# A mixing stage laid out anew: paired heads in the sparse attention, gate products between its steps, and no empty matmuls

## The reference

```python
u = rms_norm_2(h, mix_norm[i])
z = u @ w_in[i]
(aq, ak, av, iq, ik, iw, rq, rk, rv, rg, ga, gb) = jnp.split(z, split_points, axis=-1)
aq, ak, iq, ik = rope(...)                       # 8 heads of 64; ak, av, ik are one shared head
y_a = dsa_attention(aq, ak, av, iq, ik, iw, n_sel)
rq, rk = rope(...)                               # 4 heads of 128
y_r = group_norm_heads(retention(rq, rk, rv), ret_gn[i]) * jax.nn.silu(rg)
merged = jax.nn.sigmoid(ga) * (y_a @ w_branch_a[i]) + jax.nn.sigmoid(gb) * (y_r @ w_branch_b[i])
h = h + merged @ w_out[i]
```

## Time and profile before

| | us |
|---|---|
| median of the runs | 2613.55 (2613.17 to 2618.36, 3 runs) |
| span of the profiled execution | 2617.4 |
| slowest of the runs, with which that span agrees but for 1.0 | 2618.36 |
| PE busy in the profile | 2480.4 (95% of the span) |
| DVE busy | 1396.8 (53%) |
| ACT busy | 764.3 (29%) |
| POOL busy | 595.8 (23%) |

### The profile page before, as it was taken

The page is one execution under the profiler, slowest core; times in us unless marked ns, Lnnn a source line. Parts: engine busy times, 40 slices in busy tenths (PEclk is TensorE's granted clock), DMA queues, the critical chain, the costliest instruction groups (busy, mean ns, idle before and its releaser), DMA issues.

```text
span 2617.4 us, 29928 instructions
## 1 busy us (share of the span) xinstructions
PE 2480.4 (95%) x11088; PEld 1980.8 (76%) x11088; DVE 1396.8 (53%) x1951; ACT 764.3 (29%) x1204; POOL 595.8 (23%) x275
## 2 busy tenths in 40 slices
PE   6789999988999999999999999979989999999997
PEld 5677888876667788887888887566578887888886
DVE  5566444453676643446554357698435245544465
ACT  2114323321333432333322233412422113322232
POOL 6670000015446000000000005463036882000000
PEclk8899999998999999999999999989999999999999
DMA  4232333312223233332333322121012333333321
GB/s 163 73 96 65 113 97 96 97 48 80 80 72 97 65 107 102 96 98 68 106 96 98 95 82 80 41 72 48 16 39 75 96 112 91 115 101 95 86 81 53
DMA packets 64824, 221.81 MB, mean 85 GB/s; under 512 B 7504, under 2 KB 9680, under 8 KB 64592
## 3 DMA queue, kind: packets, MB, share of 16 engines
q1 hardware_dynamic: 59184, 208.17, 27.0%
q10 hardware_dynamic: 5536, 12.19, 1.4%
HBM read 218.23 MB, written 2.10 MB: 84 GB/s over the span
## 4 chain that ended last, share of the span: by engine, by line
PE 82%; DVE 11%; ACT 3%; POOL 2%; issue 2%; DMA 0%; POOLq 0%; ACTq 0%; DVEq 0%
PE PS L422 22%; PE PS L424 21%; PE PS L423 21%; PE PS L508 3%; PE PS L453 3%; PE PS L570 1%; PE PS L457 1%; DVE SS L1252 1%; POOL WL L367 1%; PE PS L584 1%; PE PS L805 1%; PE PS L717 1%; PE PS L605 1%; PE PS L738 1%; PE PS L727 1%
## 5 line engine op out<-in xcount | busy, mean ns | idle before, releaser
L422 PE MATMUL PS<-XH,WH 128*128 128x512 f32 x1600 | 633.4, 396 | 18.1 <-DVE T L1476 12.5
L424 PE MATMUL PS<-XH,WL 128*128 128x512 f32 x1632 | 637.0, 390 | 0.0
L423 PE MATMUL PS<-XL,WH 128*128 128x512 f32 x1600 | 624.1, 390 | 0.0
L364 POOL TENSOR_TENSOR WH<-RAW,ONES 128x1024 fp32r<-128x1024 f32 (+1 forms) x123 | 240.9, 1958 | 1569.8 <-DVE WL L1240 734.8
L1240 DVE TENSOR_TENSOR WL<-RAW,WH 128x1024 fp32r<-128x1024 f32 (+2 forms) x268 | 317.6, 1185 | 198.4 <-ACT WH L899 193.7
L422 PE MATMUL PS<-HH,WH 128*128 128x512 f32 x992 | 389.0, 392 | 2.6 <-DVE HL L1326 2.6
L424 PE MATMUL PS<-HH,WL 128*128 128x512 f32 x992 | 386.2, 389 | 0.0
L423 PE MATMUL PS<-HL,WH 128*128 128x512 f32 x992 | 386.1, 389 | 0.0
L422 PEld LDWEIGHTS PS<-XH,WH 128*128 128x128 f32 x1600 | 301.4, 188 | 98.3 <-issue 20.2
L899 ACT ACTIVATE WH<-RAW 128x1024 fp32r<-128x1024 f32 (+2 forms) x272 | 276.7, 1017 | 305.9 <-DVE M L1357 202.4
L424 PEld LDWEIGHTS PS<-XH,WL 128*128 128x128 f32 x1632 | 307.2, 188 | 64.9
(11 more groups left out here) (236 smaller groups left out, 2786.4 us busy)
## 6 DMA issues: line engine op xcount, KB each, us to landing
RAW<-in_weights SPq DMA_DIRECT2D x379, 512.0 KB, 3.5
RAW<-in_weights SPq DMA_DIRECT2D x16, 384.0 KB, 3.1
H<-in_xT ACTq DMA_DIRECT2D x8, 256.0 KB, 8.4
BIAS<-in_rel ACTq DMA_DIRECT2D x8, 256.0 KB, 3.5
RAW<-in_weights SPq DMA_DIRECT2D x8, 256.0 KB, 2.7
out<-R ACTq DMA_DIRECT2D x8, 256.0 KB, 2.1
BIAS<-in_rel ACTq DMA_DIRECT2D x8, 224.0 KB, 3.9
DECAY<-in_decay ACTq DMA_DIRECT2D x1, 1024.0 KB, 4.9
```

Source lines behind the costliest of these rows:

```text
L364: nc.gpsimd.tensor_tensor(high[:, 0:w], raw, ONES[:, 0:1].to_broadcast([P, w]), ALU.mult).then_inc(high_split, 1)
L422: nc.tensor.matmul(PS[:, bank_, :], high[:, w], xh[:, k, :], start=(k == 0), stop=False)
L423: nc.tensor.matmul(PS[:, bank_, :], high[:, w], xl[:, k, :], start=False, stop=False)
L424: return nc.tensor.matmul(PS[:, bank_, :], low[:, w], xh[:, k, :], start=False, stop=stop)
```

## The change

It touches the mixing stage alone. What each part does now:

- **`mix_heads`**: no empty matmuls. DVE takes a unit straight out of PSUM times the cosine (`cosine_part`; 1/rms is multiplied into the four tables once, with four multiplications at the start), ACT copies crosswise straight out of PSUM, and the bank counts as evacuated only after the sine (`sine_part`). The index scores are done in pairs on the two halves of PE's rows, behind every second tile of the last five units (`index_pair`, `beside_heads`). ACT copies the scores into the search's work area.
- **`ret_qk`**: the crosswise halves lie in PSUM (`swapped`), and three rounds of the search go with each unit instead of two.
- **`ret_v`**: 15 rounds before the first half is taken out, 9 before the second. PE goes through the half bank by bank (`half_by_banks`), each bank waiting for its own evacuation alone.
- **The retention comes before the sparse attention**, written out without loops; PE reads `R1` directly (no `KR`), the next head's scores come before the transposes, and the output's high and low parts (`RH`, `RL`) are made per head.
- **The sparse attention** has the first attention's form: 16 steps of two heads, with four tiles of the 8 gate-a units (`merge_a`, now a table row of its own) in each. In each step ACT scales the first head's probabilities and DVE the second's.
- **`merge`** is left with 24 units: gate b, branch a, branch b.
- **Weights**: POOL's last range ends at unit 295. From there to 330 ACT and DVE split (`split_behind`, and the calls in the merge), four units ahead; the units from 323 on use `WH2`/`WL2`.

```diff
-            ("ret_gate", 8), ("merge", 32), ("mix_out", 8), ("ffn_b2", 2 * FFN_B + 8 * len(groups_of(FFN_B))),
+            ("ret_gate", 8), ("merge_a", 8), ("merge", 24), ("mix_out", 8), ("ffn_b2", 2 * FFN_B + 8 * len(groups_of(FFN_B))),
-POOL_RANGES = ((0, 28), (92, 124), (256, 331))
+POOL_RANGES = ((0, 28), (92, 124), (256, 295))
```

PE's list:

```diff
-            product(DT, XH, XL)
-            keep_busy(24, 7)
-            pe.wait_ge(evacuated, v_ready)
...
-            for t in range(TT):
-                product(DT, XH, XL, after=lambda k: index_scores(8 * t + k))
+            def index_pair(m):
+                t, a = divmod(m, PAIRS)
+                if m == 0:
+                    pe.wait_ge(rotated, 5)
+                if m == 1:
+                    pe.wait_ge(index_ready, 1)
+                if m >= 2:
+                    pe.wait_ge(relu_done, 2 * m - 2)
+                for hh in range(2):
+                    r = slice(hh * HD, hh * HD + HD)
+                    nc.tensor.matmul(PS[:, 4 + m % 2 * 2 + hh, 0:n_of(t)], AQIQ[r, 4 + a, t * P:t * P + P],
+                                     IK[r, 0:n_of(t)], start=True, stop=True).then_inc(index_done, 1)
+            def beside_heads(j):
+                if j == 1:
+                    transpose_avw()
+                if j % 2 == 1 and j // 2 < TT * PAIRS:
+                    index_pair(j // 2)
+            for s in range(5):
+                product(DT, XH, XL, after=lambda k: beside_heads(s * DT + k))
+            for s in range(8):
+                product(DT, XH, XL)
+            half_by_banks()
+            half_by_banks()
...
+            ret_scores(0)
+            for h in range(4):
+                ret_gate(2 * h)
+                ret_values(h)
+                ret_gate(2 * h + 1)
+                if h < 3:
+                    ret_scores(h + 1)
+                ret_transposes(h)
...
+            for s in range(first_step, last_step + 1):
+                j = 4 * (s - first_step)
+                if s < last_step:
+                    sparse_scores(s)
+                gate_a_tile(j)
+                gate_a_tile(j + 1)
+                if s > first_step:
+                    sparse_transposes(s - 1)
+                gate_a_tile(j + 2)
+                gate_a_tile(j + 3)
+                if s > first_step:
+                    sparse_values(s - 1)
```

ACT's list, in each step of the sparse attention:

```diff
+                for hh in range(2):
+                    c = s % 2 * 2 + hh
+                    act.wait_ge(x_done, 2 * s + hh + 1)
+                    x = PROB[:, s % 2, hh, 0:n_of(t)]
+                    S.activation(x, x, ACT.Exp, bias=NMX[:, c:c + 1], scale=-1.0,
+                                 accum_out=SUMX[:, c:c + 1]).then_inc(e_done, 1)
+                act.wait_ge(sums_inverted, s - first_step + 1)
+                c = s % 2 * 2
+                x = PROB[:, s % 2, 0, 0:n_of(t)]
+                S.activation(x, x, ACT.Copy, scale=RECX[:, c:c + 1]).then_inc(first_scaled, 1)
+                if t % 2 == 1 and s > first_step + 2:
+                    split_behind((s - first_step - 3) // 2)
```

DVE's list:

```diff
+            def cosine_part(n, cos, scale):
+                if n >= 2:
+                    dve.wait_ge(rotated, n - 1)
+                V.scalar_tensor_tensor(T[:, n % 2 * 2, :], unit(), scale, cos, ALU.mult, ALU.mult).then_inc(turned, 1)
+            def sine_part(n, dst, sin, scale):
                 dve.wait_ge(act_out, ao.next())
+                V.scalar_tensor_tensor(swapped(n), swapped(n), scale, sin, ALU.mult, ALU.mult).then_inc(evacuated, 1)
+                dve.wait_ge(evacuated, FIRST["mix_heads"] + n + 1 + (n > 4) + SLOTS)
+                V.tensor_tensor(dst, swapped(n), T[:, n % 2 * 2, :], ALU.add).then_inc(rotated, 1)
...
             for n in range(8):
-                rotate(R1[:, n:n + 1, :], COS128, SIN128, 1.0 if n % 2 == 0 else P ** -0.5,
-                       lambda: take(2 * n, 2))
-            for half in range(2):
-                take(16 * (half + 1), 16)
-                token_major(half, VT)
+                scale = 1.0 if n % 2 == 0 else P ** -0.5
+                cosine_part(10 + n, COS128, scale)
+                take(3 * n, 2)
+                sine_part(10 + n, R1[:, n, :], SIN128, scale)
+                take(3 * n + 2, 1)
+            take(24, 15)
+            token_major(0, VT)
+            take(39, 9)
+            token_major(1, VT)
```

More of the change, by code:

```diff
@@ L103, in weight_slot @@
             return (u - zero) % (2 * SLOTS)
+    out = FIRST["mix_out"]
+    if u >= out:
+        return u % SLOTS + SLOTS * ((u - out) // SLOTS % 2)
     return u % SLOTS
@@ L485, in products, with half_by_banks @@
                             product(DT, xh, xl)
+            def half_by_banks():
+                first = split.n
+                for q in range(4):
+                    high, low = weights_of(split.n - SLOTS)
+                    pe.wait_ge(weights_split, split.next())
+                    if q == 0:
+                        bank.next(4)
+                    for j in range(TT):
+                        if q == 0:
+                            pe.wait_ge(evacuated, bank.now(back=TT - 1 - j))
+                        tok = slice(j * P, j * P + P)
+                        for kk in range(2):
+                            k = 2 * q + kk
+                            w = slice(kk * SEQ, kk * SEQ + SEQ)
+                            for x, wt in (XH, high), (XH, low), (XL, high):
+                                last = nc.tensor.matmul(PS[:, (first + j) % SLOTS, :], x[:, k, tok], wt[:, w],
+                                                        start=(k == 0 and x is XH and wt is high),
+                                                        stop=(k == DT - 1 and x is XL))
+                    last.then_inc(units_done, 1)
             def token_major_half(ready=None, before_last=None, high_now=None):
@@ L844, in _, with transpose_avw @@
-            pe.wait_ge(evacuated, bank.now() + SLOTS)
-            pe.wait_ge(h_ready, hr.now())
-            hr.next(DT)
-            with loop(pe, 8, [(split, 4), (bank, 4)]):
-                product(DT, XH, XL)
-                product(4, YAH, YAL)
-                product(DT, XH, XL)
-                product(DT, HH, HL, hr)
-            hr.next(DT)
-            products(MGH, MGL, hr)
-            xp.n = 9 * DT
+            avw = FIRST["mix_heads"] + 5
+            def transpose_avw():
+                pe.wait_ge(evacuated, avw + 1 + SLOTS)
+                for j in range(TT):
+                    last = nc.tensor.transpose(PS[:, 7, j * P:j * P + P], T[:, 2, j * P:j * P + P], IDENT[:])
+                last.then_inc(avw_done, 1)
@@ new lines, in branch_b_product @@
+            def branch_b_product():
+                u = split.n - SLOTS
+                pe.wait_ge(weights_split, split.next())
+                pe.wait_ge(evacuated, bank.next())
+                for k in range(DT):
+                    w = slice(k * P, k * P + P)
+                    high, low = weights_of(u)
+                    nc.tensor.matmul(PS[:, u % SLOTS, :], high[:, w], RH[:, k, :], start=(k == 0), stop=False)
+                    nc.tensor.matmul(PS[:, u % SLOTS, :], low[:, w], RH[:, k, :], start=False, stop=False)
+                    last = nc.tensor.matmul(PS[:, u % SLOTS, :].rearrange("p (t n) -> p t n", t=TT), high[:, w],
+                                            RL[:, :, w], start=False, stop=(k == DT - 1))
+                last.then_inc(units_done, 1)
@@ L856, in _ @@
+            split.n, bank.n = FIRST["merge"] + SLOTS, FIRST["merge"]
+            pe.wait_ge(evacuated, ga0 + 7 + SLOTS)
+            ya = Count(ya_low, 4)
+            for f in range(DT):
+                product(DT, XH, XL)
+                product(4, YAH, YAL, ya if f == 0 else None)
+                branch_b_product()
+            mg = Count(mg_low, DT)
+            products(MGH, MGL, mg)
+            xp.n = 8 * DT
             xr.next(DT)
@@ L1166, in _ @@
[L1166 to L1177 removed]
+            heads = FIRST["mix_heads"]
@@ new lines, in _, with relus @@
+            for n in range(5):
+                swap_halves(n, heads + n, 32)
+            def relus(first, last):
+                for n in range(first, last):
+                    t = n // 8
+                    act.wait_ge(index_done, n + 1)
+                    if n >= 4:
+                        act.wait_ge(index_added, n - 3)
+                    S.activation(RELU[:, n % 4, 0:n_of(t)], PS[:, 4 + n % 4, 0:n_of(t)], ACT.Relu)\
+                     .then_inc(relu_done, 1)
+            relus(0, 10)
@@ L1705, in _ @@
+            for u in range(FIRST["mix_out"] + SLOTS, FIRST["mix_out"] + 2 * SLOTS):
+                split_low(u)
             for t in range(DT + 1):
```

666 lines of the change are left out of this document (322 added, 344 removed).

## The result

The changed kernel took 2519.15 us, median of 4 runs (2516.17 to 2524.35), against 2615.95 for the kernel before on the same chip (4 runs). The ratio is 0.9622, with a 95% interval of 0.9599 to 0.9644: 3.8% faster, 97 us. Forecast were 2508.5, a range of 2499 to 2532, and a chance of 0.97 for faster. The time lies in the range and 10.6 above the number. Each ratio is that of undisturbed executions: of all runs here two of before_no_empties, its profiled one among them, were disturbed.

What follows compares the result with a forecast made beforehand. PE was taken as the bound except in the search, which DVE bounds. Stage gains 53.8 + 18.0 + 0 + 14.0 + 14.6 + 0 + 4.5 = 104.9 off 2613.55 gave 2508.6, stated as 2508.5; range 2499 to 2532, own range 2500 to 2516.

Steps and rivals of the forecast that it cites:

- rival 1: Index stage of `mix_heads`: DVE bounds it, two or three units held 2 to 4 us; 2515 to 2521, chance 0.20.
- Sparse attention: Sparse attention with gate a: 139.8 us falls to 86.0, priced from the first block's attention steps; gain 53.8.
- I price it at nothing: Sparse attention: moving the first head's scaling from DVE to ACT gains 0; if ACT is late, 0.5 to 1.5 us a step.
- the term for the waits: `mix_heads`: PE waits 2.1 for a bank, about 3 for the avw unit, 1 for index scores, plus 1.5 for the clock.
- I take 0 beyond the waits above: `mix_heads`: no added loss from DVE instructions held by POOL; if held and late, 2 to 4 us per affected unit.
- the last unit's rotation and its rounds 5.95: `ret_v`: DVE's work left after `ret_qk` ends, 5.95 us, before the 15 search rounds of 20.6.
- The 2.4 for the clock: `ret_v`: 2.4 us lost to a lower PE clock after the wait, between 0 and 3.5.
- Rest: Rest of the merge 0; behind `mix_out`, most of 5.0 us of idle and clock loss goes with POOL silent: gain 4.5.
- 2: Sparse attention steps fall behind PE, 0.5 to 1.5 us for each of 16 steps; 2517 to 2533, chance 0.12.
- 3: `ret_v` gains nothing, since PE waits for the same 48 search rounds wherever they stand; +14, 2522, chance 0.05.
- 4: Fewer waits than taken: index and avw waits hidden, no clock lost; 2495 to 2500, chance 0.03.
- 5: Sparse and retention steps: waits drop PE to 1.2 GHz, half speed, through both stages; +155, 2664, chance 0.02.

Runs made afterwards that it cites:

- before_no_empties: The kernel before the change with all its empty matmuls left out and nothing else changed: 2678.14 us, ratio 1.0168 to the kernel before.
- pool_light: The changed kernel with POOL splitting only 16 of 1024 columns in 12 weight units, the rest left out: 2504.0 us, ratio 0.9547 to the kernel before.
- pool_at_tail: The changed kernel with 16 added idle POOL instructions, two after each unit of `mix_out`: 2530.45 us, ratio 0.9668 to the kernel before.

## Why the prediction was right, and where it was off

The sum of the stages, 101.9 for 104.9, is closer than its terms. `mix_heads` and `ret_v` gave 10.7 less than forecast, the other stages 7.7 more, so the closeness is in part luck. Of the 10.6 by which the time is above the number, 3.0 are this sum, 2.9 the later start of the stage, and 4.6 the step from span to median: the forecast took the median 3.85 below the profiled span, and it came 0.75 above. These last two are scatter of executions. The time lies outside the forecast's own range of 2500 to 2516 (its listed bounds add up to 2502.5 to 2517) and in that of rival 1. Of the signs named, most came: 73.4 us ahead of the first sparse score, four sparse steps in 19.9, no bracket on retention scores or behind `mix_out`. The single wait of 4 to 6 around `ret_v` did not, and brackets of 0.5 and more on L774 and on products of `mix_heads`, the sign of rival 1, did.

- **Sparse attention** (53.8, measured 58.8): right in form, undersized by 5.0. The form of the first block carried over. There was no wait at the start (2 forecast) and 1.3 at the end (2.5), and the steps themselves took 79.7, not 81.5. "I price it at nothing", said of ScalarE's scaling, holds for the added work on ACT (no wait came of it), but not for the edit: without it 3.3 us are lost, because DVE's scaling is held while POOL works.
- **`mix_heads`** (18.0, measured 13.5): the term for the waits was mis-sized. The waits sum to 8.8 (1.76, 2.09, 1.03, 1.51, 0.83, 1.57) where 6.1 and 1.5 for the clock stood; the clock cost nothing. The larger miss is in the matmuls: 69.2 less 8.8 and 43.6 is 16.8 for the pairs and transposes, where 13.5 stood. Most of it is the change from a product to a pair and back, 0.16 each time: the pairs of 128 keys follow each other every 2.01 us, of which six product matmuls of 0.227 are 1.36 and the pair 0.49.
- The step that failed is "I take 0 beyond the waits above since DVE had 34.09 of 52.4 before and does about the same work now". DVE had 54.18 busy of 69.17, some 19 of it hold (the groups above and the sum of the index key, cut at 1675.9, against their means in pool_light), and another 6 on the part that it did behind the stage. Rival 1 named the cause and its price of 6 to 12, but looked for it as PE waits in the index stage. Nearly as much of it came out 50 us later: pool_light gives 7.5 in `mix_heads` and 6.0 in `ret_v`.
- **`ret_qk`** (0): right for PE. A unit's rotation and three rounds took DVE 4.9 us at 256 keys and 5.7 at 384. But DVE entered it 16.7 late and won back only a few us.
- **`ret_v`** (14.0, measured 7.8): the first term of the sum, "the last unit's rotation and its rounds 5.95", was 14.3 (the rotation ended 13.2 behind PE, its third round 1.1 later). The 15 rounds took 20.6, as forecast. The 2.4 for the clock were not lost on the path: behind a last wait of 2.90 the second half took 21.9, at a clock of 1.00. With DVE in time (pool_light) every term came: a wait of 5.37, forecast 5.5, a second half of 24.1 with its clock, forecast 24.2, and 51.7 for the stage, forecast 51.5.
- **Retention** (14.6, measured 15.2): right, no wait at any score.
- **Rest** (4.5, measured 6.4): right; 29.2 for the start of the MLP fell to 23.6 with POOL silent, and pool_at_tail brings waits back. That POOL's silence did it, and not the earlier split of the weights, is supported by that run but not isolated.
- **Rivals.** 1 was true in its cause, and its 2515 to 2521 held the time. 2 did not come. 3 was half right. 4 did not come. 5 did not come either: the sparse and retention stages have no wait above 0.83, while before_no_empties shows that such a fall does happen in the kernel before.

The chain from POOL to `ret_v` is shown from both sides (less POOL, operands in PSUM). What is argued only is how the 102 us divide between the edits of a stage. In the sparse attention, the largest term, pairing the heads and putting gate products between the steps were not tried apart. An estimate from the rows: before, the 140 empties of 0.227 were 31.8 of the 96.2, which leaves 64 for the attention's own work; now it is 79.7 - 43.6 = 36. So about half of the 58.8 would be empties replaced and half two heads in one step. Within `mix_heads` pairs, PSUM operands and the missing empties were not tried apart, and the retention's new order was not tried alone.

The port rule cited in the prediction (the Trainium skill, "SBUF — State Buffer", "SBUF: two separate sides") agrees with these runs: at 128x512, two SBUF operands took 1.20 to 1.67 us in the mean in the changed kernel, and 0.69 to 0.75 with one of them in PSUM or with POOL light.
